# Six branch products moved into the recurrence, and the second half of two output products begun during attention, in a two-block transformer kernel

## What is computed

```python
# first block, for layer 0 and 1
x = x + 0.5 * swiglu(rms_norm(x), ...)
mixed = mix_stick_moba(xn, ...) if layer % 2 == 0 else mix_forget_dilated(xn, ...)
x = x + mixed @ w_out[layer]
x = x + 0.5 * swiglu(rms_norm(x), ...)
# second block
gates = sigmoid(u[..., RW_COLS + MLA_COLS:]).reshape(B, T, 2, D)
y_rw  = rwkv7_time_mix(u_rw, ...)          # the recurrence
y_mla = mla_mix(u_mla, ...)                # latent attention
merged = gates[:, :, 0] * (y_rw @ w_br_rwkv) + gates[:, :, 1] * (y_mla @ w_br_mla)
x = x + merged @ w_out_2
x = x + peer_ffn(...)                      # 16 experts per head and token, gathered
```

## Time and profile before

| | us |
|---|---|
| median of 3 runs | 2289.1 |
| lowest, highest | 2287.0, 2296.8 |
| the profiled execution's own time | 2298.0 |
| its span, first to last instruction | 2296.2 |
| TensorE busy | 2030.1 (88%) |
| VectorE / ScalarE / GpSimd busy | 1274.1 / 805.8 / 655.2 |
| mean granted clock of TensorE | 0.955 of 2.4 GHz |

### The profile page before, as it was taken

The page is one execution under the profiler, slowest core; times in us unless marked ns, Lnnn a source line. Parts: engine busy times, 40 slices in busy tenths (PEclk is TensorE's granted clock), DMA queues, the critical chain, the costliest instruction groups (busy, mean ns, idle before and its releaser), DMA issues.

```text
span 2296.2 us, 35217 instructions
## 1 busy us (share of the span) xinstructions
PE 2030.1 (88%) x14096; PEld 1641.8 (72%) x14096; DVE 1274.1 (55%) x2330; ACT 805.8 (35%) x1336; POOL 655.2 (29%) x671
## 2 busy tenths in 40 slices
PE   7999989999999999999988999986778677668867
PEld 7999969999999988999877887872333333224425
DVE  5555635655564664654565443285666566666543
ACT  5434335444443454433663323121211222112222
POOL 0000010000000100000002322047777777777772
PEclk9999989999999999999999998998899988989998
DMA  9553506554654524654305000579999999999993
GB/s 307 195 182 118 184 1 220 181 185 146 203 172 157 174 66 136 195 188 128 126 1 178 26 21 27 181 261 369 360 397 372 361 364 367 357 369 368 363 378 145
DMA packets 254878, 489.60 MB, mean 213 GB/s; under 512 B 13936, under 2 KB 174224, under 8 KB 254624
## 3 DMA queue, kind: packets, MB, share of 16 engines
q0 software_dynamic: 73888, 268.53, 31.1%
q1 hardware_dynamic: 177104, 214.32, 28.8%
q10 hardware_dynamic: 3760, 5.02, 0.7%
HBM read 486.74 MB, written 1.05 MB: 212 GB/s over the span
## 4 chain that ended last, share of the span: by engine, by line
PE 66%; POOL 14%; DMA 6%; issue 6%; DVE 5%; ACT 3%; POOLq 0%; DVEq 0%; ACTq 0%
PE bank L763 65%; POOL arena_sb L2720 11%; POOL con_sb L2720 3%; DMA arena_sb<-peer_u,arena_sb 2%; DMA con_sb<-peer_v,arena_sb 2%; DMA arena_sb<-peer_v,arena_sb 1%; DVE parts_sb L2033 0%; PE bank L914 0%; DVE xT_sb L2097 0%; DVE parts_sb L2028 0%; DVE sq_sb L2592 0%; DVE arena_sb L2439 0%; ACT parts_sb L1558 0%; DMA xT_sb<-xT 0%; DMA ring_sb<-ffn_w_gate 0%
## 5 line engine op out<-in xcount | busy, mean ns | idle before, releaser
L763 PE MATMUL bank<-arena_sb 64*64 64x64 f32 (+7 forms) x3688 | 516.3, 324 | 156.1 <-ACT arena_sb L1984 112.6
L763 PE MATMUL bank<-xh_sb,parts_sb 128*128 128x256 f32 x3328 | 605.2, 284 | 19.6 <-DVE parts_sb L2028 16.2
L763 PEld LDWEIGHTS bank<-arena_sb 64*64 64x64 f32 (+4 forms) x3688 | 301.7, 162 | 362.2 <-issue 219.4
L763 PEld LDWEIGHTS bank<-xh_sb,parts_sb 128*128 128x128 f32 x3328 | 514.5, 190 | 25.9 <-issue 25.0
L763 PE MATMUL bank<-xl_sb,parts_sb 128*128 128x256 f32 x1808 | 509.7, 282 | 0.0
L2592 DVE CUSTOM_DVE_ANT_0 sq_sb<-arena_sb 128x1024 f32<-128x1024 f32 x256 | 309.6, 1224 | 265.8 <-DMA arena_sb<-peer_u,arena_sb 262.8
L2028 DVE TENSOR_TENSOR parts_sb<-ring_sb,parts_sb 128x2048 fp32r<-128x2048 f32 x132 | 298.7, 2290 | 174.6 <-ACT parts_sb L1544 174.6
L763 PEld LDWEIGHTS bank<-xl_sb,parts_sb 128*128 128x128 f32 x1808 | 343.5, 190 | 0.0
L2720 POOL DMA_INDIRECT arena_sb<-peer_u,arena_sb x256 | 278.0, 1086 | 196.8 <-DVE arena_sb L2540 113.0
L1544 ACT ACTIVATE parts_sb<-ring_sb 128x2048 fp32r<-128x2048 f32 x132 | 248.0, 1909 | 59.6 <-PE bank L763 58.3
L763 PE MATMUL bank<-h_high_sb,parts_sb 128*128 128x256 f32 x1408 | 255.8, 282 | 0.0
(11 more groups left out here) (273 smaller groups left out, 1871.2 us busy)
## 6 DMA issues: line engine op xcount, KB each, us to landing
ring_sb<-ffn_w_gate SPq DMA_DIRECT2D x44, 1024.0 KB, 5.4
ring_sb<-ffn_w_up SPq DMA_DIRECT2D x44, 1024.0 KB, 6.7
ring_sb<-ffn_w_down SPq DMA_DIRECT2D x44, 1024.0 KB, 5.0
ring_sb<-w_in SPq DMA_DIRECT2D x17, 1024.0 KB, 6.0
ring_sb<-w_in_ab SPq DMA_DIRECT2D x12, 1024.0 KB, 5.2
ring_sb<-w_out SPq DMA_DIRECT2D x12, 1024.0 KB, 5.2
ring_sb<-w_in_cd SPq DMA_DIRECT2D x12, 1024.0 KB, 5.3
ring_sb<-peer_w_q SPq DMA_DIRECT2D x8, 1024.0 KB, 5.3
```

The costliest lines, as they stand in the source:

```text
L763: return pe.matmul(dst, lhsT, rhs, start=start, stop=stop_, skip_group_check=loose)
```

## The change

Three things are done, and no matmul is added or taken away.

1. Six of the eight latent branch units move from `branches_out` into the waves: units 0 and 1 behind levels 5 and 6 of wave 0, units 2 and 3 the same in wave 1, unit 4 behind level 5 of wave 2, unit 5 behind level 5 of wave 3. They use bank 3, and ScalarE copies them to a buffer of their own (`MTW`). Units 6 and 7 stay, in banks 6 and 7. VectorE's product with the gates becomes two instructions (6 chunks and 2).
2. So that the first branch weights are there, their slot moves ahead of the gates' slots 5 to 7 in the ring.
3. In layers 0 and 1 the output chunks 4 to 7 (banks 2 and 3) are begun in the last three attention steps with the `MIX` chunks that are ready: 4, 8 and 8 of their 32 matmuls in layer 0, three times 8 in layer 1. What is left of them, 12 and 8 matmuls, stays at the end.

```diff
+        WAVE_BRANCH = [(0, 1), (2, 3), (4,), (5,)]
+        MTW = view(2048, 6, T)
...
+                    for m in WAVE_BRANCH[w][l - 5 : l - 4] if l >= 5 else ():
+                        plan(("br", 1, m), 3)
...
-        for m in range(8):
+        for m in (6, 7):
             plan(("br", 1, m), 4 + m % 4)
...
+            OUT_EARLY = {0: ((0,), (4, 1), (5, 2)), 1: ((4, 5), (6, 7), (0, 1)), 2: ()}
...
+            def out_early(l, i):
+
+                for kk in OUT_EARLY[l][i]:
+                    out_ready(l, kk)
+                    for m in range(4, 8):
+                        k = at["wo", l] + m // 2
+                        first = kk == OUT_EARLY[l][0][0]
+                        if first and m % 2 == 0:
+                            have(k)
+                            fill_begin(pe, ("y", l, m // 2))
+                        b = bank[fill_of["y", l, m // 2][0]]
+                        ins = mm(b[:, (m % 2) * T : (m % 2 + 1) * T], slot(k, KC, 256)[:, kk, (m % 2) * P : (m % 2 + 1) * P],
+                                 MIX[:, kk, :], first and m % 2 == 0, False, loose=True)
...
+                    if l == 1 and t >= 9:
+                        out_early(1, t - 9)
                     if t >= 4:
                         soft_mixed(l, t - 4)
...
+                    if t >= 4:
+                        out_early(0, t - 4)
                     if t >= 3:
                         soft_mixed(0, t - 3)
...
+                        for m in WAVE_BRANCH[w][l - 5 : l - 4] if l >= 5 else ():
+                            branch_part(1, m)
...
-                for branch, src in ((1, YM), (0, YR)):
...
+                for m in (6, 7):
+                    branch_part(1, m)
+                pe.wait_ge(S("y_rw_ready"), 2)
+                for m in range(8):
+                    branch_part(0, m)
+                out_product(2, MG)
```

More of the change, by code:

```diff
@@ L313, in build @@
         at["in2", 1] = k; k += IN2_SLOTS - IN2_FIRST
-        at["gates"] = k; k += 8
-        at["br"] = k; k += 4
+        for s in range(5):
+            at["gates", s] = k; k += 1
+        at["br", 0] = k; k += 1
+        for s in range(5, 8):
+            at["gates", s] = k; k += 1
+        for s in range(1, 4):
+            at["br", s] = k; k += 1
         at["wo", 2] = k; k += 4
@@ L733, in _, with gate_weights, branch_weights @@
                 in2(i)
[L734 to L735 removed]
+            def gate_weights(s):
+                k = at["gates", s]
                 fetch(k, slot(k, KC, 256), rows(w2)[:, :, 2336 + 256 * s : 2592 + 256 * s])
[L737 to L740 removed]
+            def branch_weights(s):
+                k, w = at["br", s], (A["w_br_mla_2"][0], A["w_br_rwkv_2"][0])[s // 2]
+                fetch(k, slot(k, 4, 512), rows(w)[:, :, s % 2 * 512 : (s % 2 + 1) * 512])
+            for s in range(5):
+                gate_weights(s)
+            branch_weights(0)
+            for s in range(5, 8):
+                gate_weights(s)
+            for s in range(1, 4):
+                branch_weights(s)
             square(at["wo", 2], A["w_out_2"][0], 4)
@@ L1129, in gate @@
             def gate(m):
-                k = at["gates"] + m // 2
+                k = at["gates", m // 2]
                 if m % 2 == 0:
@@ L1233, in latent, with branch_part @@
                 soft(2, 4)
+            def branch_part(branch, m):
+                src = YM if branch else YR
+                k = at["br", 2 * (1 - branch) + m // 4]
+                b = fill_begin(pe, ("br", branch, m))
+                if m % 4 == 0:
+                    have(k)
+                for kk in range(4):
+                    ins = mm(b[:, 0:T], slot(k, 4, 512)[:, kk, (m % 4) * P : (m % 4 + 1) * P], src[:, kk, :], kk == 0, kk == 3)
+                    if kk == 0:
+                        release(ins)
+                fill_end(ins, ("br", branch, m))
+                if m % 4 == 3:
+                    owed[0] += 1
             def recurrence():
@@ L1250, in recurrence @@
                              ("bonus", j))
+                for pair in range(4):
+                    emptied(pe, ("mt", 2, pair))
                 for w, (d, c) in enumerate(WAVES):
@@ L1902, in recurrence @@
                 act.activation(GATES, GATES, ACT.Sigmoid).then_inc(S("gates_ready"), 1)
-                for m in range(8):
-                    b = take(act, ("br", 1, m))
-                    give(act.activation(MT[:, m, :], b[:, 0:T], ACT.Copy), ("br", 1, m))
+                for m in (6, 7):
+                    branch_out(m)
                 act.dma_start(PIN, rows(A["pT"])).then_inc(S("p_loaded"), 16)
```

66 lines of the change are left out of this document (36 added, 30 removed).

## The result

| | before | changed |
|---|---|---|
| median of 20 runs each, us | 2295.2 | 2277.4 |
| lowest, highest | 2282.9, 2302.1 | 2271.2, 2287.6 |
| profiled execution's own time | 2298.0 | 2281.1 |
| its span | 2296.2 | 2279.3 |

The ratio is 0.9934, 95% interval 0.9919 to 0.9949: 15.1 us less than before (11.7 to 18.6). The two medians lie 17.8 us apart and the two means 14.8. The forecast was 2280.4 us with a range of 2272 to 2289, so the time lies in it, 3 us under the forecast. So the gain was under-estimated by 6 us, the starting point lay 6 us too low, and the two errors largely cancel: that the time came out so close is in part luck. The missing 6 us of gain are what the experiments had to explain.

A forecast was written before the change was run, and what follows sets the result against it. TensorE was taken as the bound, busy 88% of the span. Terms of 2.6 + 1.6 + 2.0 = 6.2 us plus 2.5 us of clock gave 8.7 us, 2289.1 to 2280.4 us, range 2272 to 2289.

The forecast's parts named there:

- Layer 0 and layer 1: Early out product matmuls fill TensorE's waits: 6.5 us in layer 0 (2.6 idle, 3.9 clock), 1.6 us in layer 1.
- the wait in front of its fall is the one that is filled: Layer 0's last steps: reason for taking the clock as staying up, about 3.9 us; if it falls, 2.6 us remain.
- the gain passes on: After layer 0's out product: the 6.6 us gain reaches the feed-forward block, which TensorE bounds; everything downstream moves as a block.
- Behind the waves: After `gvar`: 9.05 us won by moving six units, a new 3.6 us wait, 1.7 us lost to the clock.
- 0.9 us behind level 5, 1.72 behind level 6: In the waves: cost of each moved unit, four behind level 5 and two behind level 6, together 7.0 us.
- no wait to fill: Level 6 of the waves: U's operands come during TT, so a unit there costs its full 1.72 us.
- Dense matmuls just ahead of U may prevent one or both; the bounds are 0 and +3, I take +1.5.: Waves 0 and 1: units behind level 6 may prevent the clock's falls to 1.2 GHz, gaining 1.5 us.
- not each run will have had these slow stretches; on the median I count two thirds of the clock's part.: Whole kernel: the clock's 3.7 us is cut to 2.5 us for the median, making the gain 8.7 us.
- The sum: Whole kernel: 6.2 us without the clock plus 3.7 us of clock, 9.9 us on the profiled execution; 8.7 on the median.
- the clock gives all: Rival: no clock falls in layer 0, waves 0 and 1 or at the new wait; 14.7 us, 2274.4 us, chance 0.22.
- The slower rival: Waves stretched: six units at 1.2 GHz cost 3.44 us each, total 2296.5 us; slower from 2.2 us each; chance 0.05.

The follow-up runs named there:

- before_again: The kernel before, unchanged, run and profiled once more; ratio to before 0.9994.
- rec_only: The changed kernel without the early out product matmuls of layers 0 and 1, six units left in the waves; ratio to before 0.9973.
- layer0_last16: The changed kernel with nothing early in layer 1 and only the last 16 of layer 0's 20 early matmuls; ratio to before 0.9938.
- four_units: The changed kernel with four units in the waves, one behind level 5 of each, and four behind `gvar`; ratio to before 0.9909 in both series.
- four_level6: The changed kernel with four units in the waves, each behind level 6, and four behind `gvar`; ratio to before 0.9932.

## Why the prediction was right, and where it was not

**Layer 0 and layer 1: right.** 7.05 and 1.6 us against 6.5 and 1.6. The step "the wait in front of its fall is the one that is filled" was tested by itself and holds. VectorE's L2180 is not waited for. But "the gain passes on" holds only as far as layer 1: from its feed-forward row to the first gram product of wave 0 it is 343.10 us before and 344.95 after. A fall of 3.4 us at about 1095 us, in code that the change does not touch, takes 1.9 us back: the nine profiles that hold it need 344.4 to 345.6 us there, the four that do not (before, before_again, rec_only, layer0_last16) 343.0 to 343.4. The sum had no such term.

**Behind the waves: right.** The wait is 3.63 us (3.6 forecast) and 3.4 us at half rate follow it (forecast 1.7 us lost). From `gvar` to the first gather it is 83.63 us before (1427.62 to 1511.25) and 76.32 after, 7.3 us less; 9.05 - 1.7 was 7.35. That the clock goes down behind such a wait is what the Trainium skill, page "TensorE: Matmul & The Clock Gate", section "HAM oscillation — how this bites in real kernels", says. The trace agrees with that, but the work behind the wait does not start cold here: it begins at 1433.26, and the stretches have the clock at 1.00 until about 1434.5. four_units, which fills the wait, gains 9.0 us there (83.63 to 74.64), 1.7 more than six, which is what the fall was priced at. The kernel before can pay at this place too, which I had not seen in its profile: in before_again the clock falls behind the 2.29 us wait for gate 15, and it is 85.32 us (1434.47 to 1519.79).

**The price in the waves: too low.** The step "0.9 us behind level 5, 1.72 behind level 6", 7.0 us together, measured 8.9. Behind level 5 it is 1.2 to 1.3: the waits at level 6 are gone, but less than their 0.86 us comes back. Behind level 6 "no wait to fill" was right, the amount was not. In four_level6 the unit holds TensorE from 1318.14 to 1320.06:

```profile
1318.14 1.99 PE L782 MATMUL bank<-arena_sb,ring_sb 128*128 128x256 f32 x8
1320.06 5.99 PE L782 MATMUL bank<-arena_sb 64*64 64x64 f32 x64
```

that is 1.92 us for four matmuls that are 1.72 us apart in a row of their like; and ScalarE's last copy of W at level 6 and its first copy of U, 1.67 us apart before (1325.13, 1326.80), are 3.81 apart there (1317.38, 1321.19). Why the whole wave pays up to 2.5 us is not settled.

**The clock in the waves: far too low, and this is the step that failed.** "Dense matmuls just ahead of U may prevent one or both; the bounds are 0 and +3, I take +1.5." Measured: 21 us less low time in the waves, 8.9 us. The mechanism was named and its direction was right; the size came from one execution, whose waves hold 19.4 us of low time where three other profiles of the same recurrence hold 37 to 40. The prediction also counted 9 us of it only, at waves 0 and 1, and left out the fall in waves 2 and 3 (9.2 us in that profile), and took 0.3 us for one low us where pairs of profiles show 0.42. In the first pair of profiles itself the low time of the waves goes from 19.4 to 6.4 us, 5.5 us by that price; the 8.9 us rest on the average over the profiles of several kernels. The next step was wrong in sign: "not each run will have had these slow stretches; on the median I count two thirds of the clock's part." The profile showed a better execution of before than most, where the waves are concerned.

**The sum, mended.** Layers 8.6 us, the fall at 1095 us -1.9, behind the waves 7.3, price in the waves -8.9, clock in the waves +8.9: 14.0 us, against 15.1 and 14.9 measured. The two last terms cancel, so the recurrence's part pays only because of the clock: without it, it would be a loss of 1.6 us. This is an account from averages and not a reading of one pair: at the first gather the two profiles of before and of the changed kernel lie 10.6 and 11.7 us apart (1519.79 and 1508.05 for the second pair, which is of two series), so 3 to 4 us of the measured 15 stand in no pair of their profiles. Whether they come from executions of before with more low time, or from the experts' part, stays open. The same account gives 16.8 us for four units (9.0 behind the waves, -5.1 and +6.2 in them, 6.7 from the layers), and 20.3 and 21.4 were measured, with errors of 2.1 and 2.8, so something of it may be missing. Four units are the fastest version in both series where they were run, 0.9909 of before twice, and 6.5 ± 3.2 us under the changed kernel where the two stand in one series.

**The rival "the clock gives all"** (14.7 us) had the size, though not the terms: it had no fall at the new wait and +3.0 in the waves. The slower rival needed units of over 2.2 us each; they cost 1.5 on average.

## What to carry to other kernels

Where TensorE runs small dependent products that let its granted clock fall now here and now there, look at the clock in more than one execution before pricing a change: the same instructions took 173.7 to 184.0 us for four waves. Dense independent matmuls placed there can be nearly free, where they pay in clock what they cost in time, as they did here on average; stop adding them where the place they come from begins to wait, as that wait brought a fall of 3.4 us of its own here. And when a clock falls behind a chain of short waits, fill the one just ahead of the fall first: four matmuls did most of what twenty did.

## What was not expected of the hardware

- The clock fell behind a stretch in which, by the rows, TensorE was never idle. In the earlier trace rows three short waits stand ahead of the fall in wave 0; in four_units these are filled, TensorE is busy with 64x64 products for 5.40 of 5.40 us, and then the clock falls all the same:

```profile
1275.20:1280.60 5.40, 5.40 (x62) 4.46 (x61) 0.98 (x4) 2.15 (x8) 0.00 (x0) 1.00 0.00 0
1280.60:1284.00 3.40, 3.40 (x32) 3.28 (x33) 0.58 (x2) 0.28 (x1) 0.00 (x0) 0.50 0.02 5
```

  The seven profiles with a unit of four 128x256 matmuls behind level 6 of wave 0 have no fall there.
- Single falls ahead of the first gather lasted from 3.4 to 17.1 us, and each us of low time cost 0.41 to 0.46 us in the recurrence.
- A fall can move in code that was not changed. Nine of the ten profiles with early matmuls in layer 0 hold one at some 1095 us that before, before_again and rec_only do not have, and it costs 1.9 us. That the early matmuls bring it is not shown: layer0_last16 has sixteen of them and no fall. after's row is

```profile
1092.00:1098.00 6.00, 5.21 (x16) 2.21 (x16) 6.00 (x19) 4.99 (x9) 0.00 (x0) 0.72 0.21 75
```

- From the first to the last gather it took 744 and 738 us in the first pair of profiles, 747 to 756 in the first series, 727 to 740 in the second and 757 to 764 in the third. It goes with the level of the times, and each series was on another chip: the medians of before are 2292 in the second series and 2321 in the third.
